# The release that a matmul unit waits for: the third-last result in place of the second-last, in a fused two-model layer stack

## The reference

```python
def first_block(x, ...):
    h = rms_norm(x, norm_mix_g[l]);  proj = h @ w_in[l]
    ya = moba_attention(qa, ka, va)                       # 8 heads of 64
    yb = rg_lru(causal_dwconv(rx, ...), ...) * gelu(rgate)
    yc = diff_attention(qc, kc, vc, lam, lam_init, ...)   # 4 heads
    merged = g0 * (ya @ w_branch_a) + g1 * (yb @ w_branch_b) + g2 * (yc @ w_branch_c)
    x = x + merged @ w_out[l]
    u = causal_dwconv(rms_norm(x, norm_ffn_g[l]) @ ffn_up[l], ...)
    x = x + (gelu(u_gate) * u_val) @ ffn_down[l]
    return rms_norm(x, final_norm_g)

def hybrid_layer(x, ...):                                 # twice
    u_pool, q, k, v, xc, gate_b, gate_c, gate_logits = split(x @ w_in)
    o_a = multiscale_pool_mixer(u_pool, ...)
    o_b = sliding_window_gqa_sinks(rope(q), rope(k), v, sinks)
    o_c = gate_b * causal_dwconv_2(gate_c * xc, conv_w)
    merged = sum(sigmoid(gates[i]) * (o_i @ w_branch_i));  mix = merged @ w_o
    x = layer_norm(ALPHA * x + mix)
    x = layer_norm(ALPHA * x + (silu(a) * b) @ w_down)    # a, b = causal_dwconv_2(x @ w_up)
```

## Time and profile before

| | |
|---|---|
| median of 3 runs | 1332.35 us (1332.01 to 1335.2) |
| the profiled execution's own time | 1332.38 us |
| its span, first to last instruction | 1330.6 us |
| PE busy | 1242.3 us (93%) |
| DVE, ACT, POOL busy | 883.3, 716.0, 358.4 us |
| mean granted clock of TensorE | 0.969 of full speed |
| read from HBM | 210.31 MB, 159 GB/s over the span |

### The profile page before, as it was taken

One profiled execution on the slowest core, in us unless ns is written; L12 is line 12 of the kernel. 1 busy time (PEld: TensorE's weight loads), 2 busy tenths in 40 slices (PEclk: granted clock), 3 DMA queues, 4 the chain that ended last, 5 costly groups with the idle time before them and its releaser, 6 DMA issues. The chain is left out here.

```text
span 1330.6 us, 26782 instructions
## 1 busy us (share of the span) xinstructions
PE 1242.3 (93%) x9986; PEld 1198.2 (90%) x9986; DVE 883.3 (66%) x1469; ACT 716.0 (54%) x1235; POOL 358.4 (27%) x351
## 2 busy tenths in 40 slices
PE   5998989899899999899997999998999988999997
PEld 4987878799899999888997999998988987999996
DVE  5656667567677854665577777756655587777755
ACT  4654557445566644455444766643555444666543
POOL 2021100722344412130045244413110045333313
PEclk9999889999999999899999899999999998999998
DMA  6633234455466666444454465565444553565562
GB/s 239 191 112 121 87 126 127 143 191 180 148 189 189 183 185 194 141 144 139 146 167 150 143 189 190 168 189 166 139 135 140 160 158 127 169 192 191 168 190 87
DMA packets 60286, 212.67 MB, mean 160 GB/s; under 512 B 6688, under 2 KB 7968, under 8 KB 60064
## 3 DMA queue, kind: packets, MB, share of 16 engines
q1 hardware_dynamic: 60192, 211.39, 51.6%
HBM read 210.31 MB, written 1.05 MB: 159 GB/s over the span
## 5 line engine op out<-in xcount | busy, mean ns | idle before, releaser
L987 PE MATMUL bank<-xhi,whi 128*128 128x256 f32 x2368 | 685.5, 289 | 38.6 <-DVE xlo L1246 16.5
L1242 DVE TENSOR_TENSOR wlo<-raw,whi 128x1024 fp32r<-128x1024 f32 (+1 forms) x400 | 498.8, 1249 | 290.3 <-ACT whi L670 287.7
L988 PE MATMUL bank<-xlo,whi 128*128 128x256 f32 x2368 | 669.9, 283 | 0.0
L989 PE MATMUL bank<-xhi,wlo 128*128 128x256 f32 x2368 | 669.3, 283 | 0.0
L987 PEld LDWEIGHTS bank<-xhi,whi 128*128 128x128 f32 x2368 | 456.4, 193 | 60.1 <-issue 48.4
L670 ACT ACTIVATE whi<-raw 128x1024 fp32r<-128x1024 f32 (+1 forms) x400 | 415.1, 1039 | 146.4 <-PE bank L989 129.8
L988 PEld LDWEIGHTS bank<-xlo,whi 128*128 128x128 f32 x2368 | 456.4, 193 | 0.7
L989 PEld LDWEIGHTS bank<-xhi,wlo 128*128 128x128 f32 x2368 | 456.4, 193 | 0.0
L987 PE MATMUL bank<-fhi,whi 128*128 128x256 f32 x528 | 148.2, 281 | 3.7 <-DVE wlo L1242 3.7
L577 POOL TENSOR_TENSOR fprod<-ugate,uval 128x256 f32<-128x256 f32 x66 | 88.1, 1336 | 229.0 <-DVE uval L1578 209.5
L988 PE MATMUL bank<-flo,whi 128*128 128x256 f32 x528 | 147.5, 279 | 0.0
(11 more groups left out here) (197 smaller groups left out, 1250.8 us busy)
## 6 DMA issues: line engine op xcount, KB each, us to landing
raw<-in_w_win SPq DMA_DIRECT2D x140, 512.0 KB, 3.6
raw<-in_w_up SPq DMA_DIRECT2D x132, 512.0 KB, 3.6
raw<-in_w_down SPq DMA_DIRECT2D x48, 448.0 KB, 3.6
raw<-in_w_merge SPq DMA_DIRECT2D x32, 512.0 KB, 3.5
raw<-in_w_out SPq DMA_DIRECT2D x24, 512.0 KB, 3.5
raw<-in_w_down SPq DMA_DIRECT2D x24, 512.0 KB, 3.6
x<-in_x SPq DMA_DIRECT2D x4, 256.0 KB, 4.0
rgw<-in_rg_w SPq DMA_DIRECT2D x1, 1024.0 KB, 9.3
```

Source lines behind the costliest of these rows:

```text
L987: pe.matmul(ps, whi[:, slot, w], hi, start=first, stop=False)
L988: pe.matmul(ps, whi[:, slot, w], lo, start=False, stop=False)
L989: return pe.matmul(ps, wlo[:, slot, w], hi, start=False, stop=last)
L1242: dve.tensor_tensor(wlo[:, n % RING, w], raw[:, n % RING, w], whi[:, n % RING, w].bitcast(f32), ALU.subtract) \
```

## The change

`begin` gets a parameter `banks`, by default 3, and waits for `FREE[result - banks]` where it waited for `FREE[result - 2]`. `down` passes 2, as before. `merge` passes `5 - len(units[0])`: in `merge1` `units[0]` has two branches, so 3; in `merge2` it has three, so 2. So the wait is for one result further back in `win1`, `merge1`, `wout1`, `up1` and in `win2`, `wout2` and `up2` of both layers.

```diff
-            def begin(n, result, it=0, per=0, rper=0):
+            def begin(n, result, it=0, per=0, rper=0, banks=3):

                 wait(pe, split_lo, n + 1, it, per)
-                if result is not None and result >= 2:
+                if result is not None and result >= banks:

                     ahead = 0 if isinstance(it, int) else rper
-                    done, count = FREE[result - 2 + ahead]
+                    done, count = FREE[result - banks + ahead]
                     wait(pe, done, count - ahead, it, rper)
...
                     for parts in units:
-                        begin(n, r)
+                        begin(n, r, banks=5 - len(units[0]))
...
-                    begin(n, RESULT[name] + t if part == 0 else None, it, 6, 2)
+                    begin(n, RESULT[name] + t if part == 0 else None, it, 6, 2, banks=2)
```

## The result

The changed kernel takes 1324.26 us, median of 10 runs (1322.05 to 1333.16), against 1332.93 us for the kernel before (10 runs, 1330.43 to 1337.06). The ratio is 0.9943 with a 95% interval of 0.9921 to 0.9965: about 7.6 us faster (the ratios here go by the means of the runs; the medians lie 8.7 us apart). The forecast was 3.3 us, 1329.0, with a range down to 1326.0. So the direction was right, and the forecast gain was less than half of what came. A later measurement of both kernels (e10) gave 0.9932 (0.9907 to 0.9956).

What follows compares the result with a forecast made beforehand. PE, busy 1242.3 us of the span, was taken as the bound, so gains must come from its waits. Three places gave 1.0 + 1.5 + 0.8 = 3.3 us, so 1332.35 - 3.3 = 1329.0 us, range 1326.0 to 1331.5.

Steps and rivals of the forecast that it cites:

- Place 1: First input projection, 230 to 274 us, seven waits for ACT's copy: 1.0 us gain, bounds 0 and 3.0; bubbles moved, not removed.
- the term that was read at unit 63: End of the recurrence's stage in the first input projection: unit 63 starts earlier by 0.8 us.
- a chain on POOL that begins earlier: First input projection: POOL's chain can begin a little earlier because copies and weight parts come earlier, taken as 0.2 us.
- The first wait: First input projection: the 3.00 us wait ending at 230.09 with the copy of unit 50.
- Place 2: Second model's first layer, 649.63 us: unit 31 starts 2.3 us earlier, less 0.8 for pace: 1.5 us, bounds 0.6 and 2.3.
- Place 3: Second layer, 1043.48 us: unit 31 starts when its low part is there, 0.8 us earlier; bounds 0 and 1.9.
- Elsewhere: Rest of the kernel: no bank waits beyond the nine of 14.5 us; four low-weight waits stay, nothing else costs.
- A second step: Norms, merges and down projections begin when their inputs are there, so they are shifted as a whole.
- the clock falls at another place in exchange: Rival: the clock falls anyway at Place 2 or elsewhere instead, costing 0.9 or 1.7 us; 1330 to 1330.8; 20%.
- The prediction's own sign: Start of merge1: expected at about 273.0; more than 3 us earlier would show the forecast wrong.
- more than the sum: Rival: 2.72 us pace stays at Place 2 (0.8 more) and a norm's clock fall goes (1.7); 1327.5; 26%.
- all nine waits go: Rival: all nine bank waits vanish, 14.5 us, and 1.7 for the clock; 1316; 3%.
- POOL's loop get longer: Rival: in the recurrence's stage low parts lie beside two POOL steps, 0.9 us more a tile; 1336; 5%.

Runs made afterwards that it cites:

- e10: The changed kernel again, unedited, timed beside the kernel before: 1324.7 us against 1336.02, ratio 0.9932.
- e3: Changed kernel, but odd units of the up projections wait for the second-last result: ratio 0.9958 to the kernel before.
- e4: Changed kernel, but ACT makes the high part for down's third unit before the products' last high part and the table load: ratio 0.9918 to before.
- e7: Changed kernel, but even units of the up projections wait for the second-last result: ratio 0.9976 to the kernel before.
- e8: The changed kernel again, unedited, for a second profile: one run, 1327.01 us.
- e5: Kernel before, with DVE's second convolution step left out in the up projections: ratio 0.9938 to the kernel before.
- e1: Changed kernel with three banks in the up projections alone and two everywhere else: 1330.2 us against 1334.89 before, ratio 0.9971.
- e11: Repeat of e4, the early high part for down's third unit on the changed kernel: 1320.17 us, ratio 0.9881 to the kernel before.

## Why the prediction was wrong

- **Place 1** was right: 1.0 us forecast, 0.8 measured, the bubbles kept at 1.5 us and handed from L861 to L1242, and POOL's steps 4.5 us apart in the profile after as before. The 0.8 is the term that was read at unit 63. The other 0.2, for a chain on POOL that begins earlier, did not come: its first step starts 9.94 us behind unit 51 before and after. The first wait, 3.0 us, stands as 2.4 us at the next unit.
- **Place 2** was right in its mechanism: unit 31 waits 1.17 us for its low part and the clock stays at 1.00 from 640 to 655. Its size was off: I took off 0.8 us for a fast pace that would go with the clock fall. Here it didn't go (665.93 - 646.76 for seven units, 2.74 us each), and the place gave 2.2 us, near the bound of 2.3. In e3, e4, e7 and e8, with the same wait, it did go, and the place took 26.89 us, which is the forecast 1.5 us: both came, and the forecast had no means to choose.
- **Place 3**: 0.8 us forecast, 1.4 measured. The wait gave the 0.8; the rest is again pace.
- **The step that failed** is the term put at nothing under "Elsewhere": "The nine waits are all that PE shows for a bank", and before it "The up projections have no such line: there a result is freed before it is asked for." At odd units from 17 to 29 it is freed only 0.08 to 0.13 us before the unit begins, and that is not early enough; at unit 4 it is freed after PE could begin. The stall is too short to be listed, and its price is not its length but the 4% slower pace behind it, up to 39 units long. e3 and e7 show at which units it happens, and e5 that an early release avoids it; in place of nothing the up projections gave 8.0 us in the profiles and 3.9 us (1.3 to 6.5) in the times of e1. A whole projection at one or the other pace is 121.6 to 123.2 us or 126.9 to 127.8 us.
- **A second step failed** there: "Norms, merges and down projections ... are shifted as a whole." The low clock that left place 2 came back at wout2, and the stretch from unit 29 to up2 got 0.6 us longer in the profile. The rival "the clock falls at another place in exchange" named this, with 1.7 us; in the time it is covered by the gain of the up projections. The prediction's own sign, merge1 more than 3 us earlier, came true too (3.3 us), but 2.5 us of it lie ahead of place 1.
- The rival of "more than the sum" (26%) had the right sign and named the pace, but for seven units at place 2 only. I had both paces in my hands, 2.72 and 2.83, and asked what clock fall they belonged to, and not where else they change.
- The rival "all nine waits go" fell as argued: 14.1 us more of waits for low weights stand in their place. Nor did POOL's loop get longer, though the step of the first tile now takes 1.62 us and not 0.74, as foreseen.
- Not foreseen either: a faster up projection arrives at down ahead of ACT, and part of its gain can be given back there: 2.9 us in down1, 1.0 of it a longer wait and 1.7 the clock behind it. In e10, where up1 ended slow, down1 took 67.12 us as before. In e4 and e11 the long waits are gone, and down1 takes 66.9 and 66.5 us.

## What to carry to other kernels

A wait that the profile doesn't list can still cost: compare the end of each release with the start of the unit that needs it, and count instructions per window, since an engine that is 100% busy at full clock can run at two paces. Where a spare buffer exists, wait for the release that the buffer really needs; it gives little where another engine sets the pace, and it gives where the releases come just in time. Then look at the next hand-over, because the engine that runs ahead meets the next late input there, and look at the granted clock further on: here it stayed up at one place and fell at the next instead.

## What the runs showed of the hardware that I had not expected

At a granted clock of 1.00, the same stream of weight loads and 128x256 matmuls runs with a matmul every 0.113 us (885 in 100 us) or every 0.118 us (851 in 100 us), and keeps its pace for over 100 us. Stalls of about 0.1 us at units 17 to 35, and of up to 0.4 us at units 3 and 4, changed it, from fast to slow or from slow to fast; some left it (unit 17 of up1 before took 2.77 us and the next 2.72). What chooses the pace, at the start of a phase or at a stall, stays open. It also explains in part why runs of one kernel spread so far here, 1322 to 1333 us: one slow up projection is 5 us. That is an inference from the profiles, since the single runs have no trace.
